# A two-layer hybrid encoder on one core: four moves in the last stage, and a tile-by-tile end over three chunk pairs

## The reference

```python
def reference(x, norm1_g, w_in, b_f, sinks, rel_bias, w_gate, b_gate, w_br_a, w_br_b, w_br_c,
              w_out, norm2_g, w_up, conv_w, conv_b, w_down, final_g):
    h = x
    for l in range(DEPTH):
        h = h + hybrid_mixer(rmsnorm(h, norm1_g[l]), w_in[l], ...)
        h = h + conv_glu_ffn(rmsnorm(h, norm2_g[l]), w_up[l], conv_w[l], conv_b[l], w_down[l])
    return rmsnorm(h, final_g)

def conv_glu_ffn(xn, w_up, conv_w, conv_b, w_down):
    h = xn @ w_up
    s = h.shape[1]
    hp = jnp.pad(h, ((0, 0), (CONV_WIDTH - 1, 0), (0, 0)))
    hc = conv_b
    for j in range(CONV_WIDTH):
        hc = hc + hp[:, j:j + s] * conv_w[j]
    gate, up = jnp.split(hc, 2, axis=-1)
    return (jax.nn.silu(gate) * up) @ w_down
```

## Time and profile before

| what | value |
|---|---|
| median of 3 runs | 1462.41 us (1461.9 to 1462.45) |
| profiled execution, its own time | 1460.3 us |
| its span | 1458.4 us |
| PE busy | 1443.6 us, 99% |
| DVE, ACT, POOL busy | 1012.1, 700.6, 47.4 us |
| mean granted TensorE clock | 0.998 |

### The profile page before, as it was taken

The page is one execution under the profiler, slowest core; times in us unless marked ns, Lnnn a source line. Parts: engine busy times, 40 slices in busy tenths (PEclk is TensorE's granted clock), DMA queues, the critical chain, the costliest instruction groups (busy, mean ns, idle before and its releaser), DMA issues.

```text
span 1458.4 us, 19919 instructions
## 1 busy us (share of the span) xinstructions
PE 1443.6 (99%) x6983; PEld 1192.4 (82%) x6983; DVE 1012.1 (69%) x1710; ACT 700.6 (48%) x1200; POOL 47.4 (3%) x35
## 2 busy tenths in 40 slices
PE   9999999999999999999999999999999999999997
PEld 7888888888888888888888888888887888888876
DVE  7877667655777734776477776675656888888976
ACT  7655555434444422443475555553344343344665
POOL 0000000002100000000200000000020000000002
PEclk9999999999999999999999999999999999999999
DMA  6222212232322233222432222222333655555554
GB/s 250 87 73 88 87 58 74 87 102 72 130 94 93 79 98 112 101 95 72 131 121 89 86 73 80 65 80 88 122 130 116 206 180 190 211 178 186 203 166 144
DMA packets 49434, 171.38 MB, mean 118 GB/s; under 512 B 6465, under 2 KB 6593, under 8 KB 46289
## 3 DMA queue, kind: packets, MB, share of 16 engines
q1 hardware_dynamic: 45760, 147.43, 30.8%
q10 hardware_dynamic: 3600, 22.99, 4.2%
HBM read 156.70 MB, written 13.63 MB: 117 GB/s over the span
## 4 chain that ended last, share of the span: by engine, by line
PE 93%; DVE 3%; ACT 2%; DMA 1%; issue 1%; POOL 0%; SPq 0%; POOLq 0%; ACTq 0%; DVEq 0%
PE dense L784 26%; PE dense L786 26%; PE dense L785 26%; PE turned L867 2%; PE branch L894 1%; PE dense L799 1%; PE dense L801 1%; PE dense L800 1%; PE dense L1049 1%; PE dense L1051 1%; PE dense L1050 1%; PE scores L859 1%; DMA raw<-in_w_last 1%; PE scores L856 1%; PE branch L880 1%
## 5 line engine op out<-in xcount | busy, mean ns | idle before, releaser
L784 PE MATMUL dense<-hg,whi 128*128 128x512 f32 x1304 | 516.6, 396 | 3.7 <-DVE wlo L1540 3.5
L786 PE MATMUL dense<-hg,wlo 128*128 128x512 f32 x1304 | 508.9, 390 | 0.0
L785 PE MATMUL dense<-hg,whi 128*128 128x512 f32 x1304 | 508.4, 390 | 0.0
L1118 ACT ACTIVATE whi<-raw 128x1024 fp32r<-128x1024 f32 (+3 forms) x242 | 240.8, 995 | 427.2 <-PE dense L786 421.1
L1540 DVE TENSOR_TENSOR wlo<-raw,whi 128x1024 fp32r<-128x1024 f32 (+3 forms) x242 | 276.9, 1144 | 117.0 <-ACT whi L1118 115.0
L784 PEld LDWEIGHTS dense<-hg,whi 128*128 128x128 f32 x1304 | 245.5, 188 | 56.4 <-issue 5.0
L786 PEld LDWEIGHTS dense<-hg,wlo 128*128 128x128 f32 x1304 | 244.9, 188 | 52.1
L785 PEld LDWEIGHTS dense<-hg,whi 128*128 128x128 f32 x1304 | 245.3, 188 | 48.0 <-issue 0.2
L784 PE MATMUL dense<-act,whi 128*128 128x512 f32 x432 | 170.0, 394 | 0.5 <-DVE wlo L1540 0.5
L786 PE MATMUL dense<-act,wlo 128*128 128x512 f32 x432 | 168.4, 390 | 0.0
L785 PE MATMUL dense<-act,whi 128*128 128x512 f32 x432 | 168.3, 390 | 0.0
(11 more groups left out here) (317 smaller groups left out, 1610.5 us busy)
## 6 DMA issues: line engine op xcount, KB each, us to landing
raw<-in_w_up SPq DMA_DIRECT2D x88, 512.0 KB, 3.5
raw<-in_w_gate SPq DMA_DIRECT2D x48, 512.0 KB, 3.5
raw<-in_w_in SPq DMA_DIRECT2D x26, 512.0 KB, 3.5
probT<-in_w_last ACTq DMA_DIRECT2D x10, 1024.0 KB, 6.2
w_sums<-probT ACTq DMA_DIRECT2D x10, 1024.0 KB, 4.3
raw<-in_w_out SPq DMA_DIRECT2D x16, 512.0 KB, 3.5
raw<-in_w_down SPq DMA_DIRECT2D x16, 384.0 KB, 3.0
raw<-w_sums SPq DMA_DIRECT2D x8, 768.0 KB, 4.9
```

The lines of the kernel that those rows point to most:

```text
L784: mm(out, a, xhi, start=start, stop=False)
L785: mm(out, a, xlo, start=False, stop=False)
L786: return mm(out, b, xhi, start=False, stop=stop)
L1118: fn(whi[:, s, 0:cols], raw[:, r, 0:cols], ACT.Copy).then_inc(w_hi.sem, 1)
```

## The change

The first four edits are moves. (1) `residual_in` of ACT goes from behind pair 1 to behind pair 2. (2) The additions of w into u on DVE go from behind all four remainders of q = 11 to behind the first two. (3) The order of the last norm: DVE's reciprocals become steps of their own, and those of tile 3 and the bias and gain of tile 1 come before the scaling of tile 3. (4) The scaling of the left half of tile 0 and its store go from POOL and SP to ACT; SP's order of stores is a list. The fifth part: from q = 16 on three places are used in turn, and the tile-by-tile part is over q = 19, 20, 21 and not 20, 21 only.

```diff
+RING = KP + 5
...
-    return 2 if q == 2 * KP - 1 else q % 2
+    return q % 2 if q < RING else (q - RING + 2) % 3
...
+OUT_ORDER = ((2, 1, 1), (2, 0, 1), (3, 1, 2), (0, 1, 3), (3, 0, 2), (1, 1, 4))
...
-            for i, t in enumerate(LAST_ORDER):
-                for half in range(1 if i == T - 1 else 0, 2):
-                    sp.wait_ge(o_fin_v if half else o_fin_p, i + 1)
...
+            for t, half, count in OUT_ORDER:
+                sp.wait_ge(o_fin_v if half else o_fin_p, count)
...
-                for q_ in range(2 * KP - 2):
+                for q_ in range(2 * KP - 3):
...
-                ends = (2 * KP - 2, 2 * KP - 1)
+                ends = (2 * KP - 3, 2 * KP - 2, 2 * KP - 1)
...
-                            last = tile(q_, x, t, False, q_ == ends[1])
+                            last = tile(q_, x, t, False, q_ == ends[2])
...
-                if q_ == 2 * KP - 1:
-                    act.wait_ge(last_l, split_at(KP + 4, "x2"))
+                if q_ == RING:
+                    act.wait_ge(last_l, split_at(RING - 1, "x2"))
                 elif q_ >= 2:
-                    x = {"w01": "p5", "x01": "p6", "x2": "p5", "w23": "p4", "x3": "p4"}[what] if q_ < KP else order_of(q_ - 2)[-1]
-                    act.wait_ge(last_p, product_at(q_ - 2, x))
+                    before = q_ - 2 if q_ < RING else q_ - 3
+                    x = {"w01": "p5", "x01": "p6", "x2": "p5", "w23": "p4", "x3": "p4"}[what] if q_ < KP else order_of(before)[-1]
+                    act.wait_ge(last_p, product_at(before, x))
...
-                        residual_in()
                         act.wait_ge(ssum_done.sem, ssum_done.at(l, C - 1))
                         load_staged(1)
                         up_pair(l, half, 2, 0, True)
+                        residual_in()
...
-            act.wait_ge(fin_rec, T)
             act.wait_ge(fin_yg, 2)
...
+            for i, t in enumerate((1, 0)):
+                act.wait_ge(fin_rec, T)
+                fn(out_st[:, t, 0:S], y_gained[t], ACT.Copy, scale=stat[:, 1, t:t + 1]).then_inc(o_fin_a, 1)
+                act.wait_ge(o_fin_a, i + 1)
+                act.dma_start(A["out"][0, t * P:(t + 1) * P, 0:S], out_st[:, t, 0:S]).then_inc(stored, 16)
...
+                        if (q_, what) == (KP, "x01"):
+                            fold_in("u", 0)
+                            fold_in("u", 1)
...
-            def final_out(i, t):
+            def reciprocal_of(i, t):
                 dve.wait_ge(fin_root, i + 1)
                 ve.reciprocal(stat[:, 1, t:t + 1], stat[:, 0, t:t + 1]).then_inc(fin_rec, 1)
+
+            def final_out(i, t):
...
+            reciprocal_of(0, 2)
             final_out(0, 2)
             bias_of(1, 3)
             gain_left(2, 0)
             bias_of(2, 0)
+            reciprocal_of(1, 3)
+            bias_of(3, 1)
+            gain_left(3, 1)
             final_out(1, 3)
-            gain_left(3, 1)
-            bias_of(3, 1)
+            reciprocal_of(2, 0)
             final_out(2, 0)
+            reciprocal_of(3, 1)
             final_out(3, 1)
...
-            for i, t in enumerate(LAST_ORDER[0:3]):
...
+            for i, t in enumerate(LAST_ORDER[0:2]):
```

More of the change, by code:

```diff
@@ L761, in _ @@
                     load_next_first(l)
-            for i, t in enumerate(LAST_ORDER):
-                for half in range(1 if i == T - 1 else 0, 2):
-                    sp.wait_ge(o_fin_v if half else o_fin_p, i + 1)
-                    sp.dma_start(A["out"][0, t * P:(t + 1) * P, half * S:(half + 1) * S],
-                                 out_st[:, t, half * S:(half + 1) * S]).then_inc(stored, 16)
+            for t, half, count in OUT_ORDER:
+                sp.wait_ge(o_fin_v if half else o_fin_p, count)
+                sp.dma_start(A["out"][0, t * P:(t + 1) * P, half * S:(half + 1) * S],
+                             out_st[:, t, half * S:(half + 1) * S]).then_inc(stored, 16)
             sp.wait_ge(stored, 2 * T * 16)
@@ L1519, in _ @@
             root_of(3, 1)
-            act.wait_ge(fin_rec, T)
             act.wait_ge(fin_yg, 2)
-            fn(out_st[:, 1, 0:S], y_gained[1], ACT.Copy, scale=stat[:, 1, 1:2]).then_inc(o_fin_a, 1)
-            act.wait_ge(o_fin_a, 1)
-            act.dma_start(A["out"][0, P:2 * P, 0:S], out_st[:, 1, 0:S]).then_inc(stored, 16)
+            for i, t in enumerate((1, 0)):
[3 more added lines that the diff above has]
+                act.dma_start(A["out"][0, t * P:(t + 1) * P, 0:S], out_st[:, t, 0:S]).then_inc(stored, 16)
         @block.vector
@@ L1959, in down_last @@
                     if q_ == KP:
-                        for x, t in FOLDS:
-                            fold_in(x, t)
+                        fold_in("v", 0)
+                        fold_in("v", 1)
                     if q_ == KP + 3:
@@ L2140, in _ @@
             pool.wait_ge(gain_row_in, 16)
-            for i, t in enumerate(LAST_ORDER[0:3]):
[L2142 to L2147, removed]
+            for i, t in enumerate(LAST_ORDER[0:2]):
+                pool.wait_ge(fold, FOLD_AT[("c21", t - 2)])
+                nc.gpsimd.tensor_tensor(y_gained[t], y_left[t], gain_row[:, 0:S], ALU.mult).then_inc(fin_yp, 1)
+                pool.wait_ge(fin_yp, i + 1)
                 pool.wait_ge(fin_rec, i + 1)
```

## The result

The changed kernel takes 1453.81 us (1453.49 to 1454.06, 4 runs), the kernel before 1462.43 us (1461.9 to 1463.2, 4 runs), a ratio of 0.9941 with a 95% interval of 0.9923 to 0.9958. Forecast were 1456.4 us and a range of 1454.9 to 1458.4: the direction was right, the time fell 2.6 us further and out of the range. The profiled execution went from 1460.3 to 1453.72 us, its span from 1458.4 to 1451.8. So the spans differ by 6.6 us, and the medians by 8.6. That leaves two questions: where the 6.6 us went in the trace, and where 2.0 more come from that the two traces don't show.

The account below looks back on a forecast made before the run. PE bounds the kernel, so time comes from its waits, the end and its clock. Terms of 5.98 us from the profiled 1460.3 gave 1454.3, plus 2.1 for the median 1456.4; range 1454.9 to 1458.4.

Parts of the forecast that it names:

- The four terms: Gains at the residual copies, second pass, last three pairs and end: 3.62 + 1.05 - 0.44 + 1.75 = 5.98 us.
- The rival on the clock: PE's clock falls behind the new wait at 1439, starts take 0.454 us: 10.9 us more, 1467.3; chance 0.01.
- Part 1: Residual copies behind pair 2: PE's 3.46 us wait at 1123.03 goes, gain 3.62 us, bounds 1.8 to 3.7.
- Part 2: Start of second pass: w added into u early removes PE's wait at 1404.58, gain 1.05 us, bounds 0.65 to 1.1.
- Part 3: Three places and three pairs at the end: PE waits for pair 21's activations, costing 0.44 us net.
- Part 4: Behind PE's last matmul: longer tiles and new norm order shorten the end from 7.86 to 6.1 us, gain 1.75.
- the 2.86 reckoned: Last store at the end: a landing of 2.5 us and 0.36 from landing to the span's end.
- The prediction's other estimate, of 2.6 us for a landing: Last store of 256 KB: 2.0 us plus bytes over 436 GB/s, making the end 0.1 us later.
- The delay beside POOL that part 4 allowed for tokens 3: Shared port of DVE and POOL could delay the scaling of tokens 3, ending before T-1 and costing nothing.
- Part 1 coming back in part: DVE's stretch to 1144.87 is held by its own work, the 3.6 us become 1.8: 1458.2 us; chance 0.12.
- pair 21 for nothing: At the tile-by-tile end the remainder lands before PE comes, 0.97 us less: 1455.4 us; chance 0.06.
- the end not shortened: ACT's two scalings and stores replace POOL's and stores meet: gain 0.3 instead of 1.75, 1457.9 us; chance 0.1.

Follow-up runs that it names:

- the filler: Kernel before with 24 idle matmuls behind the turns of the residual: 1460.03 us; same filler in the change with the residual copies moved back: 1457.77 us.
- the earlier splits: The change, but from q = 17 on each split waits only for the product of q-3 reading the same part of the place: 1452.82 us.

## Why the prediction was wrong

The mechanisms came in the trace as forecast, each term within 0.3 us; the failed step is the last of the sum: "Against the profiled execution's own 1460.3 us (span 1458.4 and 1.9 around it): 1454.3. The median of the runs shown is 1462.41, 2.1 above the profiled one, so 1456.4." I took the 2.1 us for an offset that stays. About 1.7 of it was the price of the granted clock behind the very wait that edit 1 removes, and went with it (the filler alone took 1.85 off the median); the other 0.4 was the small group of runs, whose median lay above the 1462.0 of all 72. Without that step the forecast would have been 1454.3; with the term sizes of the traces, 1453.7. The four terms together were 0.6 us too small.

The sign of it was in view: all three runs lay at 1461.9 or above, and the profiled one 1.6 below the lowest of them. The rival on the clock leaned on the same fault. "Against it: behind the longest wait, 3.46 us, the granted clock reads 1.00 in the next microsecond, and this one is 0.9." That is true of the profiled execution, and not of the long ones; the rival then looked for the clock as a risk of the new wait of 0.9 us, and not as a cost of the old. The 0.7 us wait is followed by no loss that the runs show: the granted clock stays at 1.00 behind it, and the change spreads over 0.6 us.

Step by step:
- Part 1. Right: there is no wait, the copies have no idle time before them, and DVE's stretch moved up whole. The term was 3.62, the traces show 3.89, of which 0.12 stood already before the turns (1118.54 to 1118.42). The median shows 5.3 by edit 1 alone: 3.9 are the wait, which leaves 1.4 for the clock. The filler took 1.85 off the kernel before and 1.26 off the version without edit 1.
- Part 2. Right, 1.05 forecast, 1.17 by the traces, 1.3 by taking it back.
- Part 3. Right in place and size: wait 0.69 in the idle column, cause the split behind the last product of q = 18, shown by the earlier splits.
- Part 4. The sum was near: 1.75 forecast, 1.98 measured. The last issue came at T+3.32 for T+3.25, and from there to the end it took 2.56 us, not the 2.86 reckoned. The prediction's other estimate, of 2.6 us for a landing, rests on a fit that the Trainium skill (DMA: Bandwidth & Descriptors, Anatomy of one DMA) gives for DMAs that GpSimd issues. These stores are issued by SP and ACT, and the landings of all eight had a median of 2.1 us. The reasons for the shorter end were mixed. The three pairs with the old order shorten the end from 7.9 to 5.9 us; edits 3 and 4 with two pairs shorten it to 7.1; all together give 5.9. That doesn't make the new order idle: with three pairs, the new order and POOL kept for tokens 0 the end is 5.2. So with three pairs edit 3 brings 0.7 us in the traces (the two versions differ by edit 2 as well, which lies before the end) and edit 4 costs as much again, by two scalings and two issues in a row behind the last reciprocal. POOL's old work was no burden: with three pairs and the old order its last scaling runs from 1446.98 to 1448.55, 1.3 us past PE's end, and ACT's last scaling ends later still. What edit 3 shortens is the landing: the last issues stand 2.1 to 2.2 us behind PE's end with either order, and the longest landing is 3.2 us with the old one and 2.7 with the new. That the stores meet less is likely, but not shown.
- The delay beside POOL that part 4 allowed for tokens 3 didn't come: DVE's scaling at 1443.39 lasts 0.74 us while POOL's runs from 1442.89 to 1444.46. In the kernel before it lasted 1.27 us, begun while POOL's gain was running.
- Rivals. Part 1 coming back in part, pair 21 for nothing, the end not shortened, the clock behind the new wait: none came. What came, a cost of the clock in the kernel before, was none of them.

## What to carry to other kernels

Before a trace's own time is carried over to a median, look where it lies in the runs. If it lies below all of them, ask what the other executions do that this one doesn't, and first at the longest wait of PE. A long wait of PE then has two prices, its length and the clock behind it, and the second can be tried apart: idle matmuls in the wait. And when the last tiles are made longer, try each move of the norm alone under them: here the longer tiles brought 2.0 us, the new order 0.7 more, and one scaling moved to another engine cost the 0.7 again, which the sum of the three doesn't show.

## What was not expected of the hardware

- One wait of 3.46 us is followed by the 2.4 GHz level in some executions and by the 1.2 GHz level in others, for 5.6 us of PE's work in the trace that shows it. The 28 runs of the kernel before spread from 1460.03 to 1463.43 us and with filler by 0.5 us; the versions without such a wait spread by 0.4 to 1.8 us, of which the cause is open.
- 24 matmuls on nothing, in the wait, made the kernel before 1.85 us faster.
